# Attention scores issued in groups of two and four items in a float32 encoder layer

## What is computed

```python
h = rmsnorm(x); z = h @ w_in
q, k = rmsnorm per map (8 maps, head size 64); v: 4 heads of 128
s = q @ k.T / 8 + rel_bias[bucket]          # 512x512 (prompt) or 256x256 (sample), for 8 maps
p = softmax(s)                              # maps 2h and 2h+1 belong to head h
a = p[2h] - lam * p[2h + 1]; o = a @ v[h]
x = x + concat(rmsnorm(o) * gain, b_g * conv3(c_g * xc)) @ w_out
x = x + hierarchical_moe(rmsnorm(x))        # 16 experts, 2 per token
x = x + sigmoid(x @ w_g) * rmsnorm(p_in @ w_p)
```

## Time and profile before

| What | Value |
| --- | --- |
| Runs | 605.79 us median of 3 (604.62 to 607.21) |
| Profiled execution, first to last instruction | 603.0 us |
| Granted TensorE clock | 1.000 over the whole span |
| Busy share of the span | PE 99%, PEld 81%, DVE 70%, ACT 55%, POOL 11% |
| Chain that ended last | PE 79%, DMA 9%, DVE 6%, POOL 2%, ACT 2% |
| Chain by line | L1943 (scores) 3%, L1962 (pv) 3%, L507 to L509 58% |

### The profile page before, as it was taken

The page is one execution under the profiler, slowest core; times in us unless marked ns, Lnnn a source line. Parts: engine busy times, 40 slices in busy tenths (PEclk is TensorE's granted clock), DMA queues, the critical chain, the costliest instruction groups (busy, mean ns, idle before and its releaser), DMA issues.

```text
span 603.0 us, 8730 instructions
## 1 busy us (share of the span) xinstructions
PE 595.1 (99%) x3160; PEld 490.5 (81%) x3160; DVE 419.7 (70%) x781; ACT 329.1 (55%) x595; POOL 69.2 (11%) x109
## 2 busy tenths in 40 slices
PE   9999999999999999999999999999999999999997
PEld 6888979888888777787887887778888888888886
DVE  5523983353552565646778789899999999788863
ACT  6851030222232675656556566789999998971211
POOL 0340000000000000100100113241221221210000
PEclk9999999999999999999999999999999999999999
DMA  8945827120211412212323676999999999785611
GB/s 337 382 57 182 312 113 274 34 73 34 74 66 71 183 57 85 71 70 106 99 78 118 252 277 238 375 363 412 410 411 411 411 411 398 279 326 210 226 40 66
DMA packets 39042, 126.52 MB, mean 210 GB/s; under 512 B 6448, under 2 KB 7472, under 8 KB 38968
## 3 DMA queue, kind: packets, MB, share of 16 engines
q1 hardware_dynamic: 33224, 112.97, 51.4%
q0 software_dynamic: 4896, 12.59, 5.4%
q10 hardware_dynamic: 880, 0.41, 0.2%
HBM read 113.33 MB, written 23.10 MB: 226 GB/s over the span
## 4 chain that ended last, share of the span: by engine, by line
PE 79%; DMA 9%; DVE 6%; POOL 2%; ACT 2%; issue 1%; SPq 1%; ACTq 0%; DVEq 0%; POOLq 0%
PE bank L507 20%; PE bank L509 19%; PE bank L508 19%; PE bank L1926 7%; DMA w_raw<-in_w_in 4%; PE bank L1943 3%; PE bank L1962 3%; DMA x_T<-in_xT 2%; DMA row_scale<-x_rstd 2%; POOL bias_sb L800 2%; PE bank L537 2%; PE bank L538 2%; PE bank L539 2%; PE bank L2236 1%; PE bank L2077 1%
## 5 line engine op out<-in xcount | busy, mean ns | idle before, releaser
L502 DVE TENSOR_TENSOR w_split<-w_raw,w_split 128x1024 fp32r<-128x1024 f32 x33 | 40.5, 1230 | 22.4 <-ACT w_split L497 22.2
L507 PE MATMUL bank<-w_split,moe_xT 128*128 128x512 f32 x120 | 48.5, 404 | 0.7 <-DVE w_split L1697 0.7
L509 PE MATMUL bank<-w_split,moe_xT 128*128 128x512 f32 x120 | 47.0, 392 | 0.0
L508 PE MATMUL bank<-w_split,moe_xT 128*128 128x512 f32 x120 | 46.9, 390 | 0.0
L497 ACT ACTIVATE w_split<-w_raw 128x1024 fp32r<-128x1024 f32 x33 | 34.4, 1051 | 20.0 <-DMA w_raw<-in_w_in 19.9
L1017 ACT ACTIVATE sq_tmp<-bank 128x512 f32<-128x512 f32 x12 | 7.2, 598 | 69.2 <-PE bank L509 69.2
L984 ACT ACTIVATE s<-s,mn 128x512 f32<-128x512 f32 (+1 forms) x48 | 30.9, 645 | 19.9 <-DVE mn L1433 19.9
L486 DVE TENSOR_TENSOR w_split<-w_raw_more,w_split 128x1024 fp32r<-128x1024 f32 x32 | 38.0, 1217 | 2.7 <-ACT w_split L480 2.7
L507 PE MATMUL bank<-w_split,x3T 128*128 128x512 f32 (+1 forms) x104 | 39.4, 379 | 0.0
L509 PE MATMUL bank<-w_split,x3T 128*128 128x512 f32 (+1 forms) x104 | 38.9, 374 | 0.0
L508 PE MATMUL bank<-w_split,x3T 128*128 128x512 f32 (+1 forms) x104 | 38.8, 373 | 0.0
(11 more groups left out here) (321 smaller groups left out, 1595.2 us busy)
## 6 DMA issues: line engine op xcount, KB each, us to landing
w_raw<-in_w_moe SPq DMA_DIRECT2D x32, 512.0 KB, 15.7
w_raw_room<-in_w_moe SPq DMA_DIRECT2D x30, 512.0 KB, 16.7
w_raw_more<-in_w_moe SPq DMA_DIRECT2D x30, 512.0 KB, 17.2
w_raw<-in_w_in SPq DMA_DIRECT2D x23, 512.0 KB, 10.0
pick<-moe_rows SPq DMA_DIRECT2D x12, 512.0 KB, 5.4
bias_rows<-bias_table SPq DMA_DIRECT2D x1, 4096.0 KB
w_raw<-in_w_out SPq DMA_DIRECT2D x8, 512.0 KB, 3.4
toep<-bias_rows SPq DMA_DIRECT2D x4, 896.0 KB, 7.2
```

Source lines behind the costliest of these rows:

```text
L502: nc.vector.tensor_tensor(W[:, u % WS, 1], raw(u)[0], f(W[:, u % WS, 0]), ALU.subtract).then_inc(lo_done, 1)
L507: nc.tensor.matmul(out, hi, whi, start=first, stop=False)
L508: nc.tensor.matmul(out, lo, whi, start=False, stop=False)
L509: return nc.tensor.matmul(out, hi, wlo, start=False, stop=last)
```

## The change

The scores are issued for more than one item at a time. `SCORES_AT` says at which steps: at the even steps 2 to 14 two items, w and w+1, and at steps 16 and 20 four sample items. Items 0 and 1 go together, after the second tile of the v projection. The four items of a sample group need 256 columns each, so two of them share a bank, side by side (`scores_at`), and VectorE waits until all four are written before it reads the first. The new wait in front of item w+1 is for VectorE to have read item w-1. The lines of the changed kernel are 8 to 10 further down from there on.

```diff
+        FULL = sum(i < PROMPT_TILES for _, i in ITEMS)
+        assert FULL % 4 == 0 and all(i < PROMPT_TILES for _, i in ITEMS[:FULL])
+        SCORES_AT = {**{w: 2 for w in range(2, FULL, 2)}, **{w: 4 for w in range(FULL, NI, 4)}}
+
+        def scores_at(w):
+            return SEQS[1] * (w // 2 % 2) if w >= FULL else 0
...
                 for m in range(2):
-                    dve.wait_ge(pe_s, 2 * w + m + 1)
+                    dve.wait_ge(pe_s, 8 * (w // 4 + 1) if w >= FULL else 2 * w + m + 1)
                     dve.tensor_tensor_reduce(s_sb[w % 2][m][:, 0:nk],
-                                             bank[3 + 2 * (w % 2) + m][:, 0:nk],
+                                             bank[3 + 2 * (w % 2) + m][:, scores_at(w):scores_at(w) + nk],
...
                 if w >= 2:
-                    pe.wait_ge(d_s, 2 * (w - 1))
+                    pe.wait_ge(d_s, 2 * (4 * (w // 4) if nk < N else w - 1))
+                c0 = scores_at(w)
                 for c in range(0, nk, 256):
                     for m in range(2):
                         r = slice(m * HD, (m + 1) * HD)
-                        ins = pe.matmul(bank[3 + 2 * (w % 2) + m][:, c:c + 256], qT[i][r, h, :],
+                        ins = pe.matmul(bank[3 + 2 * (w % 2) + m][:, c0 + c:c0 + c + 256], qT[i][r, h, :],
...
-                    if b == V_B and i % 2:
-                        if i == 1:
-                            for m in range(TJ[Q_B] + 2, TJ[K_B] + TILES):
-                                t_ready(pe, m)
-                        scores(i // 2)
+                    if b == V_B and i == 1:
+                        for m in range(TJ[Q_B] + 2, TJ[K_B] + TILES):
+                            t_ready(pe, m)
+                        scores(0)
+                        scores(1)
...
-                if 2 <= w < NI:
-                    scores(w)
+                if w in SCORES_AT:
+                    for j in range(SCORES_AT[w]):
+                        scores(w + j)
```

## The result

| | before | changed |
| --- | --- | --- |
| Median of 13 runs each | 606.56 us (604.62 to 608.24) | 609.14 us (607.94 to 615.81) |
| Ratio, 95% interval | 1 | 1.0068 (1.0047 to 1.0088) |
| Profiled execution, span | 603.0 us | 607.5 us |
| Mean granted clock | 1.000 | 1.000 |

A forecast was written before the change was run, and what follows sets the result against it. TensorE was taken as the bound, busy 144.36 of 145.30 us, with waits for ScalarE and VectorE appearing once scores move. Terms 0.4 + 0.3 + 0.6 + 0.8 - 1.35 + 0.27 + 1.07 = +2.1 gave 607.9 us, range 602.5 to 610.3.

The forecast's parts named there:

- The cost of a group: Scores on TensorE: four passes cost 0.43 us, each group a fixed 0.40 us, nothing extra at item changes within it.
- That the gain is given back: Prompt and sample steps: 14 fixed costs, 5.6 us, go, but TensorE then waits for ScalarE or VectorE; net +2.1 us.
- The gain theory (the first rival): Whole stretch: TensorE is the bound, so all 5.6 us of removed fixed costs arrive, giving 600.2 us; chance 0.10.
- The new waits on `d_s`: Before item w+1, for VectorE's reading of item w-1: done over 1 us earlier everywhere, so no cost.
- Items 0 and 1, +0.4: Before step 1: 1.26 us saved, 0.86 paid earlier and 0.78 of waiting for ScalarE's v copy; net +0.4 us.
- Items 4 and 5, +0.6: Steps 4 and 5: turn_a(3) comes 0.86 us later, the copy 0.59 later, and all behind it, pv(4) too; net +0.6.
- Items 8 to 15, -1.35: Steps 8 to 15: four pairs gain 0.40 us each, less 0.12 in two where a copy comes late; net -1.35.
- Items 2 and 3, 6 and 7, 16 to 23: Waits at pv(2), mix_lo in step 7 and turn_a in the sample: +0.3, +0.8, +0.27 (16 to 19), +1.07 us (20 to 23).
- "Within 0.5%": Likeliest case for the whole kernel: 602.8 to 608.8 us, a change not told from none; 0.53 from the forecast.
- The second: Rival: sample steps keep their gain because VectorE's unbroken run of steps 17 to 19 shortens; 604.2 us, chance 0.13.
- The third: Rival: every change of item within a group costs an edge of 0.20 us, 2.8 us more; 610.7 us, chance 0.15.

The follow-up runs named there:

- the copy first: The changed kernel, with ScalarE doing the copy of the transposes ahead of exps in steps that issue no scores; 609.05 us, ratio 1.0024.
- the second comparison: The changed kernel and the kernel before run again, without edit; 610.10 us against 607.22 us, ratio 1.0039.
- the fours alone: The changed kernel with single prompt items, only the sample's two groups of four kept; 607.61 us, ratio 1.0010 to the kernel before.
- the odd pairs: The kernel before, with scores in pairs that begin at odd items, items 0 and 23 alone; 608.45 us, ratio 1.0016.
- the last kernel: The kernel before, pairing 2-3, 5-6, 7-8, 10-11, 12-13, 14-15, 18-19, 22-23, with ScalarE's transposes copy ahead of exps in steps without scores; 604.94 us, ratio 0.9957.

## Why the prediction was right or wrong

*The cost of a group*: right. 0.43 goes with four passes, and nothing arises within a group. For the fixed 0.40 the best check is the pairs 8 to 15 with the copy first: four edges go and 1.52 us with them, 0.38 each.

*That the gain is given back*: right at every place, but at items 4 and 5 by another chain than mine (see there). The gain theory (the first rival) would have had the changed kernel's stretch at 135.8, and it is 144.4. The new waits on `d_s` cost nothing, as reckoned.

*Items 0 and 1, +0.4*: this term failed. I set the end of the copy against the start on the chain of scores(1), and credited the move with all of 1.26. The timelines have it simpler. Here are the last v matmul and the first of step 1, before and, for the last v matmul, after; the first of step 1 after stands above, at 204.42:

```profile
201.47 0.39 PE L509 MATMUL bank<-w_split,h_T_prompt 128*128 128x512 f32 x1
...
202.85 0.50 PE L507 MATMUL bank<-w_split,h_T_sample 128*128 128x512 f32 x1
```

```profile
203.05 0.39 PE L509 MATMUL bank<-w_split,h_T_prompt 128*128 128x512 f32 x1
```

It takes 1.38 us before and 1.37 after. Scores(1) had been wholly free, so the move costs its full 0.86. The wait that I put at 0.78 was too short at both ends: 201.86 is 0.16 later than the place of a next projection matmul (201.70, as these come every 0.23), and from the start of the copy to TensorE's next matmul it takes 0.94 (203.48 to 204.42), not 0.74.

*Items 4 and 5, +0.6*: failed too. I took the copy of the transposes as the chain's start; it is the v projection at the end of step 4, and the term is 0.86. The copy did move by the forecast 0.6 (from 3.47 to 4.05 after scores(4)), but the second v copy, next in ScalarE's list, then waits for that projection. The idle time, which I put at 0.9 before pv(4), is 1.33 at the conv part of step 5. "All behind it, pv(4) too" was right, of a chain that starts elsewhere.

*Items 8 to 15, -1.35*: failed by 0.29, with -1.06. Single copies come late for pv, which I had put at 0.12 in two of the four pairs. With the copy first these pairs gave 1.52, so ScalarE's order is the cause.

*Items 2 and 3, 6 and 7, 16 to 23*: right to 0.12. In the sample this is luck in part. Measured between starts, less the 0.23 of a running matmul, turn_a(17), turn_a(21) and turn_a(23) wait 0.94, 1.18 and 0.93, where I had 1.18, 1.27 and 1.06; the small late places around them, which I put at 0.3 and 0.2, must have taken about as much more.

The three failed terms are short by 0.46, 0.26 and 0.29, all the same way; the others give back 0.1, and the stretch was missed by 0.9. With +3.0 instead of +2.1 my case would have stood at the 0.5% line instead of inside it.

*"Within 0.5%"*: this failed for a second reason. I took 0.5%, 3.0 us, as what the runs can tell from none. With 13 runs each the interval is 0.2% to either side, so even the 2.1 us of my own sum, 0.35%, would probably have come out clear of 1. The chance of 0.53 that I put on "the same" followed from that line. That the second comparison's 2.4 us lies near the 2.1 is luck: both traces of the changed kernel have 3.0.

*Rivals.* The first needed idle time near 1 us, and it is 6.95. The second needed VectorE's run to shorten, and it did by 0.15 us of 5.47; the fours alone cost 1.18. The third fell with the 1.93.

## What to carry to other kernels

In this kernel, removing an edge between full-height and half-height matmuls paid only where the work that was moved away had covered nothing. Look for what starts right when that work starts, and how long after it the next wait ends. If the distance between the work's neighbours would be as long without it as with it (1.37 and 1.38 us here), the work is free where it stands, and moving it to a place without a wait costs its full time. A reckoning of a bare step has to follow every engine's queue, and what stands behind each moved or late instruction, not only the longest chain: that was missed here in items 4 and 5, in items 8 to 15, in the odd pairs and in the last kernel, each time with ScalarE's list in it.

## What was not expected

Steps repeat to 0.05 us from trace to trace over 140 us, while the same code ahead of them moved scores(0) by up to 1.9 us (189.29 to 191.16) at a granted clock of 1.00, and by 3.0 in the trace of the odd pairs (192.26), whose clock was 0.96 from 40 to 80 us and 1.00 in the stretch. Small effects here are read from one stretch of a trace, not from the time.
